# Softmax and linear attention output products regrouped by the tile shape they use on TensorE, and two PSUM banks exchanged

## The reference

```python
def token_mixer(u, w_in, b_in, gla_w_a2, gla_b_a2, gla_norm_w, swa_sinks, w_out):
    z = u @ w_in + b_in
    q_a, k_a, v_a, g_a, lr_a, q_b, k_b, v_b = jnp.split(z, points, axis=-1)
    log_a = jax.nn.log_sigmoid(lr_a @ gla_w_a2 + gla_b_a2) / 16.0
    # 4 heads, key width 64, value width 128, chunks of 64 tokens:
    #   o = tril(q_dec @ k_inv.T) @ v + q_dec @ S,   S = decay * S + k_end.T @ v
    o_a = gla_chunked(q_a, k_a, v_a, log_a)
    o_a = o_a * rsqrt(mean(o_a**2)) * gla_norm_w * silu(g_a)
    # 8 query heads on 2 key-value heads of width 64; a chunk of 64 queries sees its own
    # chunk of keys and the one before, with ALiBi and a sink logit:  o = softmax(...) @ v
    o_b = swa_sink_alibi(q_b, k_b, v_b, swa_sinks)
    return jnp.concatenate([o_a, o_b], axis=-1) @ w_out
```

## Time and profile before

| | us |
|---|---|
| median of 3 runs | 2069.37 (2069.13 to 2072.68) |
| the profiled execution, its own time | 2076.87 |
| its span, first to last instruction | 2075.0 |
| TensorE busy | 1883.8 (91%) |
| DVE, ACT, POOL busy | 619.9, 511.2, 230.6 |
| mean granted TensorE clock | 0.954 |

### The profile page before, as it was taken

One profiled execution on the slowest core, in us unless ns is written; L12 is line 12 of the kernel. 1 busy time (PEld: TensorE's weight loads), 2 busy tenths in 40 slices (PEclk: granted clock), 3 DMA queues, 4 the chain that ended last, 5 costly groups with the idle time before them and its releaser, 6 DMA issues.

```text
span 2075.0 us, 30283 instructions
## 1 busy us (share of the span) xinstructions
PE 1883.8 (91%) x11006; PEld 1335.0 (64%) x11007; DVE 619.9 (30%) x1155; ACT 511.2 (25%) x1173; POOL 230.6 (11%) x319
## 2 busy tenths in 40 slices
PE   7899999999999999999983799999999999999800
PEld 4556665666656666566652688888878778888600
DVE  1333223331333223331336222222222222222265
ACT  1333332332333332333330111111111111111111
POOL 0000001000110101000001100000000001000075
PEclk9999999999999999999986899999999999999955
DMA  9322022211222022210217479888988888888576
GB/s 327 112 82 82 11 71 81 81 49 32 81 81 81 12 68 81 81 64 23 74 61 271 165 267 315 292 287 304 317 306 275 309 302 296 301 294 298 193 259 225
DMA packets 194452, 358.53 MB, mean 173 GB/s; under 512 B 12147, under 2 KB 81412, under 8 KB 194420
## 3 DMA queue, kind: packets, MB, share of 16 engines
q1 hardware_dynamic: 183780, 320.93, 45.2%
q0 software_dynamic: 10640, 37.17, 5.7%
HBM read 280.73 MB, written 77.33 MB: 173 GB/s over the span
## 4 chain that ended last, share of the span: by engine, by line
PE 86%; issue 5%; DVE 3%; POOL 2%; ACT 1%; DMA 1%; SPq 1%; POOLq 0%; DVEq 0%; ACTq 0%
PE bank L279 17%; PE bank L1071 12%; PE bank L1096 11%; PE bank L1060 11%; PE bank L425 10%; PE bank L285 7%; PE bank L1045 3%; PE bank L274 3%; PE bank L388 2%; PE bank L392 2%; PE bank L347 1%; PE bank L1085 1%; PE bank L370 1%; PE bank L372 1%; PE bank L435 1%
## 5 line engine op out<-in xcount | busy, mean ns | idle before, releaser
L279 PE MATMUL bank<-w_in_sb,uT 128*128 128x512 f32 (+1 forms) x1024 | 380.5, 525 | 17.7 <-DVE qk_sb L605 15.6
L279 PEld LDWEIGHTS bank<-w_in_sb,uT 128*128 128x128 f32 x1024 | 176.8, 192 | 187.6 <-issue 165.0
L1060 PEld LDWEIGHTS bank<-xT,wts 128*128 128x128 f32 x2048 | 252.6, 194 | 24.1 <-issue 18.1
L1060 PE MATMUL bank<-xT,wts 128*128 128x128 f32 (+2 forms) x2048 | 257.7, 286 | 4.4 <-issue 3.3
L1071 PE MATMUL bank<-xT,wts 128*128 128x128 f32 (+2 forms) x2048 | 247.9, 282 | 0.0
L1071 PEld LDWEIGHTS bank<-xT,wts 128*128 128x128 f32 x2048 | 245.0, 191 | 0.0
L1096 PE MATMUL bank<-wts,hT 128*128 128x512 f32 x512 | 233.5, 599 | 0.0
L425 PE MATMUL bank<-w_out_sb,mixT 128*128 128x512 f32 x512 | 222.4, 592 | 0.8 <-ACT mixT L503 0.8
L1124 DVE TENSOR_TENSOR hT<-bank,sg 128x256 f32<-128x256 f32 x128 | 54.4, 425 | 438.7 <-PE bank L1071 438.7
L425 PEld LDWEIGHTS bank<-w_out_sb,mixT 128*128 128x128 f32 x512 | 96.0, 190 | 115.8 <-issue 114.8
L1096 PEld LDWEIGHTS bank<-wts,hT 128*128 128x128 f32 x512 | 92.1, 190 | 99.6 <-issue 97.6
(11 more groups left out here) (206 smaller groups left out, 1876.7 us busy)
## 6 DMA issues: line engine op xcount, KB each, us to landing
wts<-w_gate_in SPq DMA_DIRECT2D x32, 2048.0 KB, 9.6
wts<-w_up_in SPq DMA_DIRECT2D x32, 2048.0 KB, 8.6
wts<-w_down_in SPq DMA_DIRECT2D x32, 2048.0 KB, 10.7
y_dram<-nought SPq DMA_DIRECT2D x64, 512.0 KB, 5.9
y_dram<-y SPq DMA_DIRECT2D x32, 512.0 KB, 10.0
x_sb<-x_in SPq DMA_DIRECT2D x17, 512.0 KB, 3.9
w_in_sb<-w_in_in SPq DMA_DIRECT2D x4, 2048.0 KB, 12.4
h_sb<-x_in SPq DMA_DIRECT2D x16, 512.0 KB, 6.1
```

The source lines that it names most:

```text
L279: m = pe.matmul(bk[name][:, col:col + hi - lo], uT[:, k, :], w_in[:, k, lo:hi], start=k == 0, stop=k == KD - 1)
L1060: m = pe.matmul(G[m_ % 2][:, 0:w], wg[:, k, m_ * P:(m_ + 1) * P], xT[:, k, 0:w], start=k == 0, stop=k == KD - 1)
```

## The change

Five things change.

1. **og**: the four whole-array products (L370) come first, then all eight 64 by 64 products. Only the first product in each bank still has start set. Both banks are waited for at the beginning, and both are signalled at the end.
2. **ob**: the output's place is now by key-value group: group gg is written to partitions 64gg to 64gg+63, head pairs a to bank ob{a}. One product serves two heads that share keys, so it has 256 moving columns; there are four over the tile's own keys and then four over the keys ahead, in place of eight and eight alternating.
3. ScalarE's copy of ob reads 128 partitions by 256 columns and writes every second block of `mixT`.
4. The rows of `w_out` are loaded to match: three transfers in place of one (2 MB on 128 partitions, twice 1 MB on 64).
5. v and router exchange their places in `JOBS`, so v has bank 1 and router bank 0. TensorE's order stays: v is still issued before router.

```diff
-    ("dS1", 1, {"S_ready": (1, 1)}), ("v", 0, {"v_ready": (1, 1)}),
-    ("router", 2, {"logits_ready": (1, 1)}),
+    ("dS1", 1, {"S_ready": (1, 1)}), ("router", 2, {"logits_ready": (1, 1)}),
+    ("v", 0, {"v_ready": (1, 1)}),
...
-        sp.dma_start(w_out[:, :, :], A["w_out"][0].rearrange("(k p) n -> p k n", p=P)).then_inc(sem("w_out_loaded"), 16)
+        sp.dma_start(w_out[:, 0:HA, :], A["w_out"][0, 0:VA, :].rearrange("(k p) n -> p k n", p=P)).then_inc(sem("w_out_loaded"), 16)
+        for gg in range(2):
+            rows = A["w_out"][0, VA + gg * 4 * HD:VA + (gg + 1) * 4 * HD, :]
+            sp.dma_start(w_out[gg * HD:(gg + 1) * HD, HA:KD, :], rows.rearrange("(c p) n -> p c n", p=HD)).then_inc(sem("w_out_loaded"), 16)
...
+        if on("og0") and on("og1"):
+            wait(pe, sem("att_ready"), 2 * (i - 1) + 2)
+            wait(pe, sem("Smid_ready"), i)
+            for hh in range(HA):
+                pr, a = hh // 2, hh % 2
+                pe.matmul(bk[f"og{a}"][:, pr * DV:(pr + 1) * DV], attm[:, hh, :], v[:, 1 - par, hh * DV:(hh + 1) * DV],
+                          start=pr == 0, stop=False, skip_group_check=True)
+            for pr in range(2):
+                o = slice(pr * DV, (pr + 1) * DV)
+                for a in range(2):
                     r = slice(64 * a, 64 * a + 64)
-                    pe.matmul(bk[name][:, o], attm[:, hh, :], v[:, 1 - par, hh * DV:(hh + 1) * DV],
-                              start=True, stop=False, skip_group_check=True)
...
+                    if pr == 1:
+                        m.then_inc(sem("og_done"), 1)
...
+        if on("ob0") and on("ob1"):
+            wait(pe, sem("pT_ready"), 3 * i)
+            wait(pe, sem("vlo_ready"), i - 1)
+            first_tile = isinstance(i, int) and i == 1
+            for a in range(2):
+                for gg in range(2):
+                    m = pe.matmul(bk[f"ob{a}"][gg * HD:(gg + 1) * HD, 0:2 * P], vb[:, 1 - par, gg * HD:(gg + 1) * HD],
+                                  pTc[:, 4 * gg + a:4 * gg + 4:2, :], start=True, stop=first_tile, skip_group_check=True)
+                if first_tile:
+                    m.then_inc(sem("ob_done"), 1)
+            if not first_tile:
+                for a in range(2):
+                    r = slice(64 * a, 64 * a + 64)
+                    for gg in range(2):
                         vp = vlo[:, gg * HD:(gg + 1) * HD] if a == 0 else vb[64:128, par, gg * HD:(gg + 1) * HD]
-                        m = pe.matmul(bk[name][r, pr * P:(pr + 1) * P], vp, pTp[r, pr, :],
+                        m = pe.matmul(bk[f"ob{a}"][gg * HD:(gg + 1) * HD, 0:2 * P], vp, pTp[r, 2 * gg:2 * gg + 2, :],
                                       start=False, stop=True, skip_group_check=True)
-                m.then_inc(sem("ob_done"), 1)
+                    m.then_inc(sem("ob_done"), 1)
...
-                r = slice(64 * a, 64 * a + 64)
-                act.activation(mixT[r, 4:8, :].rearrange("p a b -> p (a b)"), BK[f"ob{a}"][r, :], ACT.Copy)\
+                act.activation(mixT[:, 4 + a:8:2, :], BK[f"ob{a}"][:, 0:2 * P].rearrange("p (a b) -> p a b", a=2), ACT.Copy)\
                     .then_inc(sem("ob_taken"), 1)
```

More of the change, by code:

```diff
@@ L215, in clear_y @@
                 sp.dma_start(dst, src).then_inc(sem("y_cleared"), 16)
-    FIRST, CONSTS, W_OUT = 5 * 16, 11 * 16, 5 * 16
+    FIRST, CONSTS, W_OUT = 5 * 16, 11 * 16, 7 * 16
     rider = (sem("first_consts"), FIRST)
@@ L369, in pe_iter @@
                     r = slice(64 * a, 64 * a + 64)
-                    pe.matmul(bk[name][:, o], attm[:, hh, :], v[:, 1 - par, hh * DV:(hh + 1) * DV],
-                              start=True, stop=False, skip_group_check=True)
-                    pe.matmul(bk[name][0:64, o], qdkiT[r, pr, 0:64], S[r, 1 - par, pr, :],
+                    pe.matmul(bk[f"og{a}"][0:64, o], qdkiT[r, pr, 0:64], S[r, 1 - par, pr, :],
                               start=False, stop=True, skip_group_check=True)
-                    m = pe.matmul(bk[name][64:128, o], qdkiT[r, pr, 64:128], Smid[r, pr, :],
+                    m = pe.matmul(bk[f"og{a}"][64:128, o], qdkiT[r, pr, 64:128], Smid[r, pr, :],
```

## The result

The changed kernel takes **1983.8 us** (median; 1980.7 to 1985.4), the kernel before, beside it, 2071.0 (2069.1 to 2073.5): a ratio of **0.957** (95% interval 0.956 to 0.959). That is faster by 87.2 us by the medians and by 91.5 by the two profiled executions (2076.87 and 1985.40), where 100.0 were predicted. The time lies 14.4 us above the 1969.4 predicted. It is inside the wide range of 1962 to 1987, and outside the 1965 to 1977 that the prediction gave to its own mechanism.

A forecast was written before the change was run, and what follows sets the result against it. TensorE's queue was the bound, busy 65.52 of 66.31 us per iteration. Savings of 92.1 (loop), 3.15 (first tile), 1.8 (iteration 0) and 2.9 (last tile) sum to 100.0, taking the 2069.4 us median to 1969.4; range 1962 to 1987.

The forecast's parts named there:

- its own mechanism: Main forecast for TensorE's mixer path: savings of 100.0 us, giving 1969.4 us, 1965 to 1977; chance 70%.
- the two slower rivals: Column halves not overlapping in ob (1982 us, 11%), or mixA becoming the wait (1983 us, 9%).
- og, ob and v: TensorE stages in the loop: 1.50, 4.19 and 0.89 us saved per tile, 6.58 together, 92.1 over 14 tiles.
- the change of shape: TensorE: each switch between product shapes on the array costs 0.146 us.
- The first rival: ob: column halves don't overlap, 0.86 us more in 15 tiles, 13 us, 1982 us; chance 11%.
- The clock: Behind og and ob: granted clock drops to 1.2 GHz, each tile 6.6 us longer, 2168 us; chance 2%.
- The second rival, mixA: Behind og: ACT's or POOL's part takes 2 us longer against 1.2 slack, 12 to 15 us, 1983 us; chance 9%.
- Iteration 0: Pipeline start: v starts earlier, TensorE waits 3.3 us for g's weights, clock may cost 1.7; 1.8 us saved.
- Iteration 1: First tile of attention: og 1.50, ob 0.50 and v 1.15 us, together 3.15 saved.
- The last tile: Iteration 16, without kv: TensorE stands 2.6 us for mixA, so 2.9 us saved and not 5.7.
- The stages behind the mixer only move forward: Everything behind the mixer starts earlier; no gain or loss of its own was counted there.
- T3: Theory formed for the experiments: the loss in the experts comes from data, such as weight-transfer timing, or chance between executions.

The follow-up runs named there:

- swap_only: Kernel before with only the banks of v and router exchanged: 2059.7 us, ratio 0.992.
- experiment 4: Changed kernel plus 113 increments, all of ob's own-key products on the left half of the columns: 1989.8 us, ratio 0.961.
- experiment 5: Changed kernel plus 113 increments, POOL's reciprocal root of og computed three times: 1992.8 us, ratio 0.961.
- experiments 1 and 2: Both kernels rerun (2072.3 and 1985.4 us); semaphore increments between mixer and routing: 113 in the changed kernel, 1975.3 us; 143 in the kernel before, 2086.3 us.
- after_pad113: Changed kernel with 113 semaphore increments on TensorE between mixer and routing: 1975.3 us, ratio 0.952.
- before_again: Kernel before, unchanged, measured and profiled again: 2072.3 us, ratio 0.999.
- the parts: Kernel before with one part each: bank exchange 2059.7 us; og regrouped 2048.0 us; ob regrouped plus 113 increments 2015.3 us.
- one_half: Changed kernel plus 113 increments, ob's own-key products of both groups on the left half of the columns: 1989.8 us, ratio 0.961.
- before_pad143: Kernel before with 143 semaphore increments on TensorE between mixer and routing: 2086.3 us, ratio 1.005.
- merged_late_pad176: Changed kernel with ob's keys-ahead products before its own-key products, its waits as own instructions behind og, and 176 increments: 1994.1 us, ratio 0.962.

## Why the prediction was right, and where it wasn't, point by point

**The bound.** TensorE's queue was the bound and still is: 59.80 of 59.80 us busy.

**The range.** My own mechanism had 1965 to 1977; the time came in the part of 1962 to 1987 that stood there for the two slower rivals, and neither of them happened. That the range held is luck. With the code behind the mixer in its old place the change takes 1975.3 us, which the mechanism's own range does hold.

**og, ob and v.** Predicted 1.50, 4.19 and 0.89; measured 3.04 - 1.58 = 1.46, 5.77 - 1.61 = 4.16, and 1.47 - 0.61 = 0.86. Sum 6.48 for 6.58. Over the loop it is 89.88 / 14 = 6.42, so 2.2 us fewer than the 92.1. The term that was short is the change of shape: I took it at 0.146 us from ob's rhythm, and the three 64 by 64 groups (og's second, ob's second and dS) take 0.02 to 0.04 more each; ob's first group took the 1.01 predicted. The rest comes with the exchange of the banks, which makes every second iteration about 0.1 us longer, in swap_only as in the changed kernel; why is open.

**The first rival** fell by the timeline, and experiment 4 gives its price: 0.87 a tile for 0.86 predicted, and 12.6 us up to the experts for 13. The rule of the Trainium skill ("TensorE: Matmul & The Clock Gate", Part 3, What overlaps and what doesn't), that a weight load overlaps only with products of another row group, doesn't hold for two halves of the columns here: 1.01 us against 1.88. The eight weight loads of ob's first group stand at 506.51 to 507.14, inside its products (506.51 to 507.59), and all of them share their rows. **The clock** rival fell too: the window of the iteration has a granted clock of 1.00.

**The second rival, mixA.** The chain of after in the timeline, from og's squares to the gate:

```profile
506.61 0.28 ACT L487 ACTIVATE junk<-bank 128x128 bf16<-128x128 f32 x1 [6.62 <-PE bank L377]
...
507.90 0.19 POOL L721 TENSOR_SCALAR ss<-ss 128x4 f32<-128x4 f32 x1 [6.94 <-ACT junk L487]
...
508.18 1.02 POOL L723 TENSOR_TENSOR ss<-ss,neghalf 128x4 f32<-128x4 f32 x1
...
509.23 0.75 DVE L658 TENSOR_TENSOR mixA<-bank,ss 128x256 f32<-128x256 f32 x2 [3.41 <-POOL ss L723]
...
510.02 0.69 DVE L663 TENSOR_TENSOR mixA<-mixA,gm 128x512 f32<-128x512 f32 x1
```

mixA is ready at 510.71, 4.13 us behind og's last record (4.2 predicted), and asked for at 511.97: 1.26 us of slack, for 1.2 predicted and 1.17 by experiment 5.

**w_out** cost nothing, as predicted: its three transfers land 15.8 to 19.7 us after their issues at 31.4, 34.1 and 35.0, so before 55, and the first wo comes behind 88.8.

**Iteration 0**: predicted 1.8, got 0.64. The hole ahead of g came, with 2.66 us for 3.3 predicted:

```profile
31.62 8.68 PE L282 MATMUL bank<-w_in_sb,uT 128*128 128x512 f32 x16 [2.66 <-DMA w_in_sb<-w_in_in]
```

but g started 0.5 us later than the 31.1 worked out and took 8.52 us to kv at 40.14, not 6.87. Of the up to 1.7 us that I had for the clock, all was lost. **Iteration 1** paid it back: 4.29 us for the 3.15 predicted, since v took 8.36 us in place of the 9.98 of the earlier trace rows, more of it at the higher clock (granted 0.85 over v, 0.71 before). v started 1.02 us behind dS, where I had counted 0.575. og and ob there gave 1.96 of the 2.0 predicted. The two together: 4.93 for 4.95, which is luck: the two misses cancel.

**The last tile.** Predicted 2.9. wo starts 4.57 us earlier than the loop alone would give. Part of it is that dS and router ran more at the higher clock than before: from dS's start to the end of the router's records 3.98 us in place of 5.38 (966.69 to 970.67 after, 1061.52 to 1066.90 before; granted 0.94 and 0.50 in 966.69 to 970.50 and 1061.50 to 1067.00). Then wo takes longer:

```profile
979.18 0.63 PE L277 MATMUL bank<-ident,mixA 128*128 128x128 f32 x4 [2.67 <-DVE mixA L663]
980.59 15.50 PE L430 MATMUL bank<-w_out_sb,mixT 128*128 128x512 f32 x32 [0.78 <-ACT mixT L507]
```

The idle time of 2.67 us is the 2.6 predicted. The step that I left out is what comes behind it: wo took 13.97 us in the earlier trace rows, at a granted clock of 1.00 by the windows, and takes 15.50 at 0.90. The net is 3.0, right by luck in its parts.

**"The stages behind the mixer only move forward"** is the step that failed. The experts lost 6.4 us, by the place of their code (experiments 1 and 2); T3 fell with after_pad113, which has all the same data and transfers of data. I had read the instructions that the change removes as time alone, not as code that shifts what is behind it.

**From the profile to the median.** I took 7.5 us off, the distance of before's profiled execution from the first three runs. After's profiled execution lies only 1.6 us above its median, and 7.5 - 1.6 = 5.9 of the 14.4 us come from that step; 1.9 come from the mixer and the routing, 6.4 from the experts and 0.3 from the combination (14.5 by the rounded terms). The profile of before_again, 7.7 us shorter than that of before, reaches the experts at the same time (1157.82 for 1157.88): 1.5 of the 7.7 lie in the experts and 6.1 in the combination. So the distance was not a property of the kernel but where one run fell in its scatter, behind the mixer.

**What stays open.** Which places of the code are good. Counted from the kernel before, place 0 (before, the parts, and the kernels that are filled up with 112 or 113 increments) has one hole (one_half, whose chunks differ, has a second of 1.0 us); -113 (after), +143 (before_pad143) and +64 (merged_late_pad176) have five, at the same chunks. So -113 and +143 don't single out a period of 256, since +64 looks the same: it may be that place 0 is the exception. Why a fetch comes too late is only argued. For it speak the transfers, of which one starts 0.4 to 3.5 us ahead of every hole in all the traces, and the program: a chunk's gate products are the first work that follows the branch to the code of a chunk's width. Against a simple reading speak the transfers without a hole. No run removes the branch. Why the combination takes 104.5 to 110.6 us in executions of the same kernel was not tried.

## What to carry to other kernels

Where TensorE is the bound, group products by the part of the array that they use, alternate parts inside a group, and let one wider product serve the heads that share an operand: read the price of a change of shape from the start-to-start distances, as here 0.36 us against 0.215. Then ask of each group's first reader how much slack is left in its chain, and price the idle time at the ends of the pipeline with the work behind it at the lower clock. When the number of instructions changes, compare the stages that you did not touch between the two traces, and look at "issue" idle time beside the instruction packets before you explain a loss there by data.

## What the runs showed of the hardware beyond what was expected

**Code has a place, and the place costs about 10 us.** 113 increments more made a kernel 10.1 us faster; 143 made another one's experts 9.6 us slower, beyond the 4.7 us that they took themselves; 64 more made those of a third 11.9 us slower. A hole is 0.8 to 3.2 us, ahead of the first gate product of a chunk, 0.4 to 3.5 us behind the start of a 16 KB transfer on the instruction queue. Three different places of the code (after, before_pad143, merged_late_pad176) have it at the same five chunks.

**Both halves of the columns, all rows, at once**: 8 records of 256 columns on 128 by 64 in 1.01 us alternating, 1.88 on one half.

**Products on free parts of the array seem to start ahead of their turn.** In og the four records of a round start within 0.02 us, at 505.91 to 505.93, and the next four only at 506.07 to 506.09. In ob of the kernel before, the two records of a product stand next to each other. If they do so in og's program too, which the merged view doesn't show, then the second record of the first product starts behind the first records of the three products behind it.

**An increment costs TensorE about 0.15 us** once nothing covers it: 9.9 us for 64, and 4.5 us for the 30 by which before_pad143 has more than after_pad113 (18.5 and 14.0 us ahead of the rank products).
